# New order tables for the mixing work beside a gather-fed expert loop: tiles evicted one half later, taps by pairs of channel tiles, Silu, and sigmoids as tanh of half the argument

## The reference

```
xn = RMSNorm(x);  z = xn @ w_in -> u (512) | p, q (512 each) | gate logits (2048)
A  = GLU(gelu(S5 state-space layer(u)))            # GLU: pa * sigmoid(qa)
B  = silu(LayerNorm(causal depthwise conv of width 31 (p * sigmoid(q)))) @ w_conv_out
x  = x + (sigmoid(g_A) * A + sigmoid(g_B) * B) @ w_out
x  = x + PEER(RMSNorm(x))   # 8 heads; per token and head the 16 best of 128 x 128 experts:
                            # sum over the experts of softmax weight * gelu(u_e . x) * v_e
y  = RMSNorm(x)
```

## Time and profile before

| | |
|---|---|
| runs | 3581.5, 3581.9, 3587.0 us (median 3581.9) |
| the profiled execution | 3598.55 us, of which its span 3596.6 us |
| busy | PE 3197.2 us (89%), DVE 2433.1 (68%), ACT 1409.6 (39%), POOL 1401.1 (39%) |
| TensorE clock granted | 0.962 of full on the mean |
| moved by DMA | 1336.42 MB, 1140.92 MB of it gathers |
| ACT table loads | 1283 ns each; 94 in the group at L905 alone |

### The profile page before, as it was taken

How to read it: one execution, slowest core, us unless ns; L and a number is a source line. 1 busy time by engine, 2 the same in 40 slices (tenths; PEclk the granted TensorE clock), 3 DMA queues, 4 the chain that set the end, 5 groups by cost and what they waited for, 6 DMA issues and landing times.

```text
span 3596.6 us, 33769 instructions
## 1 busy us (share of the span) xinstructions
PE 3197.2 (89%) x10016; PEld 1828.4 (51%) x10016; DVE 2433.1 (68%) x5507; ACT 1409.6 (39%) x4197; POOL 1401.1 (39%) x1240
## 2 busy tenths in 40 slices
PE   7888999999999998999999998999999877777776
PEld 6676555555555555555655555555655322322232
DVE  6633579777656689777656588777666666666674
ACT  4312444554333344554333444554333333333332
POOL 1101445333343444333333344434333444454443
PEclk9899998999999998999999998999999999999999
DMA  4257998999999998999999997999999999999998
GB/s 135 72 169 239 380 418 334 367 419 379 419 405 417 410 405 321 376 410 389 419 405 404 404 407 291 389 409 400 419 409 405 409 420 420 394 420 414 414 403 348
DMA packets 232071, 1336.42 MB, mean 372 GB/s; under 512 B 27664, under 2 KB 49296, under 8 KB 92624
## 3 DMA queue, kind: packets, MB, share of 16 engines
q0 software_dynamic: 156672, 1140.92, 78.0%
q1 hardware_dynamic: 62992, 179.96, 13.7%
q10 hardware_dynamic: 12224, 13.38, 1.0%
HBM read 1310.93 MB, written 23.23 MB: 371 GB/s over the span
## 4 chain that ended last, share of the span: by engine, by line
PE 61%; DMA 20%; ACT 8%; DVE 5%; issue 5%; POOL 1%; POOLq 0%; SPq 0%; DVEq 0%; ACTq 0%
PE ps_acc L757 33%; DMA rows<-in_experts,idx 19%; PE ps_a L593 15%; PE ps_v L593 5%; PE ps_a L668 3%; DVE rows L1363 2%; ACT uy L814 2%; POOL rows L1509 1%; PE ps_y L635 1%; ACT coef L908 1%; ACT diag L912 1%; PE ps_a L695 1%; DVE va L1208 1%; ACT L905 1%; PE ps_a L672 1%
## 5 line engine op out<-in xcount | busy, mean ns | idle before, releaser
L757 PE MATMUL ps_acc<-rows,diag 128*128 128x512 f32 x4352 | 2052.8, 620 | 319.8 <-ACT diag L912 316.6
L1509 POOL DMA_INDIRECT rows<-in_experts,idx x1088 | 1272.5, 1170 | 1878.4 <-PE ps_acc L757 1516.9
L1363 DVE CUSTOM_DVE_ANT_0 rows<-rows,xn 128x1024 f32<-128x1024 f32 x1088 | 1331.1, 1233 | 845.8 <-DMA rows<-in_experts,idx 832.4
L757 PEld LDWEIGHTS ps_acc<-rows,diag 128*128 128x128 f32 x4352 | 839.9, 198 | 1370.3 <-issue 862.7
L905 ACT ACTIVATE act_v<-dots 128x2 f32<-128x2 f32 x544 | 109.8, 202 | 1170.0 <-DVE dots L1363 1158.2
L912 ACT ACTIVATE diag<-pk,coef 128x128 f32<-128x128 f32 x1088 | 377.2, 394 | 17.7
L593 PE MATMUL ps_a<-xnT,ring 128*128 128x272 f32 x1536 | 375.1, 400 | 0.9 <-ACT xnT L802 0.7
L593 PEld LDWEIGHTS ps_a<-xnT,ring 128*128 128x128 f32 x1536 | 297.5, 194 | 93.1 <-issue 35.0
L908 ACT ACTIVATE coef<-act_v,soft 128x1 f32<-128x1 f32 x1088 | 261.4, 287 | 17.8
L593 PE MATMUL ps_a<-gates,ring 128*128 128x272 f32 x1024 | 247.7, 395 | 4.2 <-issue 3.4
L1208 DVE SCALAR_TENSOR_TENSOR va<-va,pk 128x302 f32<-128x302 f32 x480 | 247.1, 579 | 1.9
(11 more groups left out here) (224 smaller groups left out, 2240.6 us busy)
## 6 DMA issues: line engine op xcount, KB each, us to landing
ring<-in_slabs SPq DMA_DIRECT2D x256, 512.0 KB
rows<-in_experts,idx POOLq DMA_INDIRECT x1088
ring<-made_slabs SPq DMA_DIRECT2D x24, 512.0 KB
sc<-score_rows SPq DMA_DIRECT2D x68, 128.0 KB
score_rows<-gp ACTq DMA_DIRECT2D x32, 256.0 KB
xt<-in_x_prompt SPq DMA_DIRECT2D x4, 1024.0 KB
x_rows<-xt ACTq DMA_DIRECT2D x4, 1024.0 KB, 11.6
x2t<-x_rows SPq DMA_DIRECT2D x8, 512.0 KB
```

The lines of the kernel that those rows point to most:

```text
L757: ins = pe.matmul(ps_acc[:, h, :], diag[:, slot, :], rows[:, slot, D + h * 512:D + (h + 1) * 512], start=first, stop=False, skip_group_che ...
L1363: ins = dve.tensor_tensor_reduce(rows[:, slot, 0:D], rows[:, slot, 0:D], xn[:, :], 1.0, 0.0, ALU.mult, ALU.add, dots[:, s:s + 1])
L1509: pool.indirect_dma_start(out=rows[:, slot, :], out_offset=None, in_=experts, in_offset=bass.IndirectOffsetOnAxis(ap=idx[:, a, k:k + 1], a ...
```

## The change

The two tables are rewritten and get a field `lag`, 0 for the opening, 1 for steady groups: ACT evicts `u`, `cq`, `gate`, `glu`, `out`, `q` and `score` tiles `lag` halves after PE made them. The taps are issued in 32 units of two taps on two of the four channel tiles, so that tiles 0 and 1 can start before `cp` 2 and 3 are there; no tap unit stands in a half that has a turn and scan. The S5 outputs are spread: three halves apart in the opening (before two), and at 20, 24, 32, 36 in a steady group (before 26, 28, 30, 32). `OPEN` is 59 instead of 60. Scores 0 are loaded one query slab earlier, scores 1 and the rows of the first tile one slab later.

Every sigmoid of the gates and of both GLUs becomes tanh(x/2): sigmoid(x) = (1 + tanh(x/2))/2. DVE forms (1 + tanh) times the other factor in one `scalar_tensor_tensor` in place of a `tensor_tensor`; the halves are taken up in conv_w, b_gate, norm_ffn, the `out` eviction, a factor 0.5 in the merge, and an identity times two (`eye2`) for the residual. The swish is one Silu on ACT, straight into `cs`, eight instructions a group, in place of four sigmoids on ACT and twelve instructions on DVE.

```diff
-    def __init__(self, pe, other, streamed):
-        self.pe, self.other = pe, other
+    def __init__(self, pe, other, streamed, lag):
+        self.pe, self.other, self.lag = pe, other, lag
...
@@ -108,36 +108,39 @@
 
 OPENING = Plan(
     {"xn": [0], "u": [1, 2, 3, 4], "cq": [5, 7, 9, 11], "cp": [6, 8, 10, 12],
-     "s": [10, 12, 14, 16], "y": [14, 16, 18, 20],
-     "gate": [13 + m for m in range(10)] + [31 + m for m in range(6)], "glu": [23 + j for j in range(DT)],
-     "mean": [32], "var": [34], "cout": [38, 39, 40, 41], "out": [43 + j for j in range(DT)],
-     "rows": [52, 53, 54], "q": [51 + m for m in range(2 * HEADS)],
-     "score": [52 + m for m in range(2 * HEADS)]},
+     "s": [10, 12, 14, 16], "y": [15, 18, 21, 24],
+     "gate": [13 + m for m in range(13)] + [34 + m for m in range(3)], "glu": [26 + j for j in range(DT)],
+     "mean": [29], "var": [32], "cout": [37, 38, 39, 40], "out": [42 + j for j in range(DT)],
+     "rows": [51, 52, 53], "q": [50 + m for m in range(2 * HEADS)],
+     "score": [51 + m for m in range(2 * HEADS)]},
     {"cp": [7, 9, 11, 13], "turn_in": [11, 13, 15, 17], "scan": [11, 13, 15, 17], "turn_back": [11, 13, 15, 17],
-     "gelu": [15, 17, 19, 21], "tap": [15 + k // 2 for k in range(TAPS)], "glu": [24 + j for j in range(DT)],
-     "centre": [33], "square": [33], "eps": [35], "root": [35], "scale": [36], "swish_in": [36], "swish": [37],
-     "cout": [39, 40, 41, 42], "rows": [53, 54, 55], "sq": [55], "ms2": [56], "rs": [57],
-     "load_x": [60], "sq_next": [64], "ms_next": [65], "norm_next": [66]}, False)
+     "gelu": [16, 19, 22, 25], "tap": [10, 10, 12, 12, 14, 14, 16, 16] + [18 + u // 2 for u in range(24)],
+     "glu": [27 + j for j in range(DT)],
+     "centre": [30], "square": [30], "eps": [33], "root": [33], "scale": [34], "swish": [35],
+     "cout": [38, 39, 40, 41], "rows": [52, 53, 54], "sq": [54], "ms2": [55], "rs": [56],
+     "load_x": [59], "sq_next": [63], "ms_next": [64], "norm_next": [65]}, False, 0)
 STEADY = Plan(
-    {"xn": [0], "u": [17, 19, 21, 23], "cq": [1, 5, 9, 13], "cp": [3, 7, 11, 15],
-     "s": [20, 22, 24, 26], "y": [26, 28, 30, 32],
-     "gate": [25 + 2 * m for m in range(10)] + [44] + [61 + 2 * m for m in range(5)],
+    {"xn": [0], "u": [9, 11, 21, 23], "cq": [1, 5, 13, 17], "cp": [3, 7, 15, 19],
+     "s": [12, 16, 24, 28], "y": [20, 24, 32, 36],
+     "gate": [25 + 2 * m for m in range(10)] + [44, 54] + [61 + 2 * m for m in range(4)],
      "glu": [45 + 2 * j for j in range(DT)],
-     "mean": [52], "var": [58], "cout": [71, 73, 75, 77], "out": [80 + 2 * j for j in range(DT)],
-     "rows": [95, 97, 99], "q": [96 + 2 * m for m in range(2 * HEADS)],
-     "score": [97 + 2 * m for m in range(2 * HEADS)]},
-    {"cp": [5, 9, 13, 17], "turn_in": [22, 24, 26, 28], "scan": [22, 24, 26, 28], "turn_back": [22, 24, 26, 28],
-     "gelu": [27, 29, 31, 33], "tap": [18 + k for k in range(TAPS)], "glu": [47 + 2 * j for j in range(DT)],
-     "centre": [54], "square": [55], "eps": [60], "root": [61], "scale": [62], "swish_in": [63], "swish": [65],
-     "cout": [73, 75, 77, 79], "rows": [97, 99, 101], "sq": [101], "ms2": [102], "rs": [104],
-     "load_x": [106], "sq_next": [117], "ms_next": [119], "norm_next": [121]}, True)
+     "mean": [48], "var": [54], "cout": [68, 70, 72, 74], "out": [77 + 2 * j for j in range(DT)],
+     "rows": [94, 96, 98], "q": [93 + 2 * m for m in range(2 * HEADS)],
+     "score": [95 + 2 * m for m in range(2 * HEADS)]},
+    {"cp": [6, 10, 18, 22], "turn_in": [14, 18, 26, 30], "scan": [14, 18, 26, 30], "turn_back": [14, 18, 26, 30],
+     "gelu": [21, 25, 33, 37],
+     "tap": [11, 12, 13, 15, 16, 17, 19, 20, 21, 22, 23, 24, 25, 27, 28, 29] + [31 + u for u in range(16)],
+     "glu": [48 + 2 * j for j in range(DT)],
+     "centre": [51], "square": [52], "eps": [57], "root": [58], "scale": [60], "swish": [62],
+     "cout": [70, 72, 74, 76], "rows": [96, 98, 100], "sq": [101], "ms2": [102], "rs": [104],
+     "load_x": [106], "sq_next": [117], "ms_next": [119], "norm_next": [121]}, True, 1)
...
 SKEW = 4
-OPEN = 60
+OPEN = 59
...
+        eye2 = sb("eye2", [P, P])
...
@@ -492,11 +495,11 @@
                     sp.wait_ge(made_stored, 96)
                 mix(h, 0)
 
-                if h == OPENING.pe["q"][5]:
-                    for b in range(2):
+                for b in range(2):
+                    if h == OPENING.pe["score"][2 * b + 1] + 2:
                         sp.wait_ge(score_out[b], 32)
                         load_scores(0, b)
-                if h == OPENING.pe["q"][7]:
+                if h == OPENING.pe["q"][8]:
                     sp.wait_ge(rows_out, 32)
                     sp.wait_ge(rs_out, 48)
                     load_rows(0)
...
 
             def mix(h, g):
-                at, due = plan(g).at, plan(g).due
-                for _ in at("xn", h):
+                due = plan(g).due
+
+                def at(piece, h):
+                    return plan(g).at(piece, h - plan(g).lag)
+
+                for _ in plan(g).at("xn", h):
                     to_channels(a_at(g, "xn"), "norm_mix", g)
                 for m in at("u", h):
                     cross(uS[:, m, :], ready(a_at(g, "u", m)), ACT.Copy, False).then_inc(a_done, 1)
                 for j in at("cq", h):
                     if j >= 2:
                         v_emptied(v_at(g, "cp", j - 2))
-                    act.activation(sig[:, j % 2, :], ready(a_at(g, "cq", j))[:, 0:N], ACT.Sigmoid).then_inc(a_done, 1)
+                    act.activation(sig[:, j % 2, :], ready(a_at(g, "cq", j))[:, 0:N], ACT.Tanh, scale=0.5).then_inc(a_done, 1)
                 for m in at("gate", h):
-                    act.activation(gates[:, m, :], ready(a_at(g, "gate", m))[:, 0:N], ACT.Sigmoid,
-                                   bias=par("b_gate")[:, m:m + 1]).then_inc(a_done, 1)
+                    act.activation(gates[:, m, :], ready(a_at(g, "gate", m))[:, 0:N], ACT.Tanh,
+                                   bias=par("b_gate")[:, m:m + 1], scale=0.5).then_inc(a_done, 1)
...
-                for _ in due("swish_in", h):
+                for _ in due("swish", h):
+                    act.wait_ge(y_done, CT * (g + 1) + 2)
                     act.wait_ge(ln_ready, g + 1)
                     for c in range(CT):
-                        act.activation(sq[:, c, :], acc[:, c, :], ACT.Sigmoid, bias=par("ln_b")[:, c:c + 1],
-                                       scale=par("ln_g")[:, c:c + 1]).then_inc(ln_sig, 1)
+                        out, shape = by_step(cs[:, c, :]), (par("ln_b")[:, c:c + 1], par("ln_g")[:, c:c + 1])
+                        act.activation(out[:, :, 0:KP], in_time(acc[:, c, 0:NP]), ACT.Silu, bias=shape[0], scale=shape[1])
+                        act.activation(out[:, :, KP:NK], in_time(acc[:, c, SOFF:NC]), ACT.Silu, bias=shape[0],
+                                       scale=shape[1]).then_inc(cs_ready, 1)
...
             def setup_angle():
 
                 dve.wait_ge(kept_in, 16)
-                dve.tensor_copy(tails[:, :, HALO:2 * HALO], par("cache").rearrange("p (c k) -> p c k", c=CT))
+                dve.tensor_scalar(tails[:, :, HALO:2 * HALO], par("cache").rearrange("p (c k) -> p c k", c=CT), 2.0, None, ALU.mult)
+                dve.tensor_scalar(par("conv_w"), par("conv_w"), 0.5, None, ALU.mult)
+                dve.tensor_scalar(par("b_gate"), par("b_gate"), 0.5, None, ALU.mult)
+                dve.tensor_scalar(par("norm_ffn"), par("norm_ffn"), 0.5, None, ALU.mult)
+                dve.tensor_scalar(eye2[:, :], par("eye"), 2.0, None, ALU.mult)
...
-            def tap(k):
-
-                taps = par("conv_w")
-                for c in range(CT):
-                    src, wk = vbuf[:, c, k:k + NC], taps[:, c * TAPS + k:c * TAPS + k + 1]
-                    if k == 0:
-                        before[c] = mark(dve.tensor_scalar(acc[:, c, :], src, wk, par("conv_b")[:, c:c + 1],
-                                                           ALU.mult, ALU.add))
-                    else:
-                        after(before[c])
-                        last = dve.scalar_tensor_tensor(acc[:, c, :], src, wk, acc[:, c, :], ALU.mult, ALU.add)
-                        if k < TAPS - 1:
-                            before[c] = mark(last)
-                if k == TAPS - 1:
+            def tap(unit, g):
+
+                taps, (two, first) = par("conv_w"), divmod(unit, 16)
+                if first == 0:
+                    emptied(v_at(g, "cp", 2 * two + 1))
+                for k in range(2 * first, min(2 * first + 2, TAPS)):
+                    for c in (2 * two, 2 * two + 1):
+                        src, wk = vbuf[:, c, k:k + NC], taps[:, c * TAPS + k:c * TAPS + k + 1]
+                        if k == 0:
+                            before[c] = mark(dve.tensor_scalar(acc[:, c, :], src, wk, par("conv_b")[:, c:c + 1],
+                                                               ALU.mult, ALU.add))
+                        else:
```

(30 more changed lines are left out.)

23 lines of the change are left out of this document (12 added, 11 removed).

## The result

The changed kernel takes 3492.5 us (median of 4 runs, 3491.4 to 3493.2) against 3581.7 us (median of 4 runs, 3570.3 to 3587.0): a ratio of 0.9755, 95% interval 0.9731 to 0.9778. Forecast were 3505 us and a range of 3474 to 3546. The profiled execution took 3491.98 us, of which its span is 3489.9 us. Lines of the changed file are higher by 3 to 17: L593 is L596, L757 is L760, L814 is L817, L845 is L852, L905 is L915, L1363 is L1375, L1509 is L1521.

The account below looks back on a forecast made before the run. A PE chain bounds the opening to the first gather, then transfers, with three dents where the DMA engines idle. Opening 34 us plus dents 43 us make 77 off 3581.9: 3505 us, range 3474 to 3546.

Parts of the forecast that it names:

- the likeliest case: The forecast itself, with shorter opening and shallower dents in the steady groups: 3485 to 3520 us, chance 57%.
- (1): Opening, gates and outputs 1 to 3: outputs three halves apart cut PE's waits; 22 us won, bounds 13 and 30.
- (2): Opening, LayerNorm: four slabs between `var` and `cout` leave 1.0 us of wait; 9 us won, bounds 5 and 10.
- (3): Opening: scores 0 loaded one slab earlier, 3.7 us won; first tile's rows a slab later cost 0, at worst 2.
- (4): Opening: four more small DVE instructions before the first normalisation, minus 0.9 us.
- (5): Steady groups: lag 1 and spread outputs end the gelu wait; y turn 14.0 us on PE, no PSUM bank missing.
- (6): Steady groups: DVE's taps overrun in turns with a scan; 6 us a group remain, at worst 12, at best none.
- the DVE rival: DVE stays the limit in the dents, 16 us of each remain: 3535 us, chance 15%.
- the slower one: Taps alternating between two channel tiles wait on each other, decisive from 0.78 us a tap: 3650 us, chance 8%.
- (7): DVE's `scalar_tensor_tensor` for `tensor_tensor`: 0 to 0.1 us on 48 instructions, offset by 12 swish instructions that go.
- (8): Silu holds ACT for about 2.9 us and two loads, hidden by the transfers.
- the loads stay: Tanh shares no table set with gelu, so each gelu keeps its 1.28 us load: 3521 us, chance 18%.

Follow-up runs that it names:

- the run with all three: Changed kernel with three opening edits: gate 12 in half 26, inverse roots and first rows earlier, silu at half 34 instead of 35; 3469.2 us, ratio 0.9681.

## Why the prediction was right, and where its sizes were off

**The sum.** 3505 us forecast, 3492.5 measured: sign, size and the likeliest case hold, but by two errors of opposite sign, 10 us too much for the opening and 22 too little for what comes behind it. That they came to 12 together was luck. The lower end of the range, 3474, lies 4 us below what its own terms give (43 and 61 off 3581.9 are 3478).

**(1) Gates and outputs, 22 forecast, 18 measured.** `glu` 0 starts at 156.02 behind thirteen gate slabs, before at 163.27 behind ten: 7.3 + 3 x 3.68 = 18.3 us. The waits came as worked out. The clock was mis-sized: 2 us were set aside, and behind output 1 alone it cost 3.3 (17.7 us to output 2, where output 2 to 3 takes 14.4); another 2.7 came behind this step's end, in `glu` 0. One load stayed, 1.4 us, since the tanh before the first gelu ran from a set without gelu.

**(2) LayerNorm, 9 forecast, 3 measured.** The wait before `cout` fell from 7.6 us to 2.5, not to 1.0: the wrong term is the silu's price, 0.72 us for a pair, from rows of other shapes, where a pair takes some 1.05. `cout` fell from 16.99 to 16.55 us and not to 14.7, since the clock fell again. The wait alone does not explain that: behind the same 2.47 us `cout` took 14.93 us with the gate moved and with Sigmoid. And 2.7 us of the 5.1 won in the wait were lost ahead of it, in the slow matmuls of `glu` 0 (4.00 + 2.70 us for what takes 2.00 + 2.00).

**(3) Scores 3.7, (4) setup minus 0.9: 2.8 forecast, 3.0 measured** (`out` starts 21.3 us earlier, the first gather 24.3), within what its place varies. But the rows of the first tile, which the same step put at 0, at worst 2, cost some 8 (8.5 us behind the first gather in the run that moves them alone, 8.3 in the run with all three). The step said that the next user waits for a gather too. The rows show that it did not: the first dot, at 325.25, waits for no gather, only for the normalisation, and this for the small load, which took 14.75 us beside the gathers. It is the step that failed outright.

**(5) Lag and outputs.** The y turn was right: 13.2 us from 579.67 to 592.89, against 14.0 forecast and 19.0 before; a turn that has an `s` piece beside the y piece takes 15.0 (524.05 to 539.05). No steady output waits for its gelu any more. The clock did not stay everywhere: the turn before the one shown has a wait of 4.09 us for diagonals and takes 16.3 us, and the share of the stretch is 1.01 all the same. A bank was missing for long only once: of the 15.2 us that PE's slabs from `gates` ever wait, 14.4 are the one wait at 325.25, for an eviction of ACT, which stood before the load of the inverse roots for 15.6 us. These rows are from PE's timeline:

```profile
524.05 3.83 PE L596 MATMUL ps_a<-xnT,ring 128*128 128x272 f32 x16
...
539.05 3.83 PE L596 MATMUL ps_a<-xnT,ring 128*128 128x272 f32 x16
...
579.67 3.83 PE L596 MATMUL ps_a<-xnT,ring 128*128 128x272 f32 x16
...
592.89 3.83 PE L596 MATMUL ps_a<-xnT,ring 128*128 128x272 f32 x16
```

What was wrong is the frame: "what happens elsewhere to ACT, DVE or PE is hidden under transfers, whose bytes don't change". The lag is worth 67 us, and a third of it lies in halves with a share of 1.01. That ACT's place costs time there is measured (23 us); by what path is argued only: a later diagonal means a later free slot and so a later transfer. Nor is all of it hidden from the share. The packets of all queues took 94.9% of the span in the repetition of the changed kernel and 94.5% in the run without the lag of `out`, `q` and `score`, 3312 and 3318 us: of the 21 us between the two profiles some 6 are longer packets and 15 idle engines, each good to some 7 us. Spread over three groups, idle time of that size hardly stands out in any one window.

**(6) Taps and scans.** The residue of 6 us a group is not to be seen: the shares of the dents are 0.99 to 1.01. The row of the taps says 584 ns, before 579; so the DVE rival (15%) is out, and so is the slower one (8%), whose chain over two tiles would have shown as 0.78 us and more. The old halves with the lag cost 19 us: spreading was worth less than the lag. The prediction had put a price on neither alone.

**(7), (8)** were not taken out one by one, so that they cost nothing is not shown.

**The rival "the loads stay" (18%)** fell with its premise. ACT's table loads, from the groups of instructions:

```profile
L915 ACT ACT_TABLE_LOAD x40 | 51.3, 1283 | 2.8 <-DVE dots L1375 2.1
L907 ACT ACT_TABLE_LOAD x34 | 43.6, 1283 | 0.6
...
L817 ACT ACT_TABLE_LOAD x1 | 1.3, 1283 | 0.0
```

87 in all, before 240. Once gelu's set is loaded (104.47), gelu follows tanh without a load, and tanh follows Silu without one (205.58), so in this build tanh is in the sets of both. The Trainium skill ("ScalarE: Activation LUTs", section on table sets) lists tanh with exp and with sigmoid, and gelu as a set of its own. For the step from tanh to gelu that is not the whole list, and the trace decides. What loads at every gelu would have meant for the time was measured with Sigmoid: 4 to 9 us, and not the 16 of that rival, as loads under transfers cost nothing that can be measured (3189.5 us from the first gather, against 3186.8).

**Open.** The packets of all queues took 92.9% of 3596.6 us before, 3341 us, and 94.9% of 3489.9 after, 3312 us, for the same bytes. So of the 107 us between the two profiles some 77 are less idle time and 29 are shorter packets. (The shares are rounded to 0.1% for each queue, so such a figure is good to some 7 us.) The two runs with lag 0 have 3334 and 3344 us, the lag on the kernel before 3325, and all the others between 3308 and 3322: the shorter packets go largely with the lag. By what means was not tested. Open are also what besides a wait decides whether PE's clock falls, and 8 to 13 us that the rest of the edit costs.

## What to carry to other kernels

In a stream in order, evict a product one step after the step that makes it: an engine that waits for its own step's product holds up everything queued behind it. Here this was worth 67 us with the rest of the change in place, and some 40, for four of the pieces, without it. Don't take a DMA share near 1 as proof that waits are free; compare the GB/s of two traces over the same work and the share of the whole run, and take the wait away as a trial. And small loads belong ahead of the first burst of gathers, even if their user seems to wait for the gathers too.

## What the runs showed of the hardware

- Tanh needs no table load behind gelu or Silu, nor gelu behind such a tanh (the first gelu behind tanh, at 104.47 us, did need one); 87 loads in place of 240, 1283 ns each.
- A load issued 4.5 us behind the first of eight gathers of 1 MB landed after 14.75 us; issued 1.4 us ahead of them it was there before DVE was ready for it, 10 us later.
- The same 1336 MB took between 3308 and 3344 us of packet time in 14 profiles with the same transfers (each figure good to some 7 us).
- After a PE wait of 4.1 us eight matmuls of 272 columns took 4.00 us, after one of 0.46 us 2.10 us. But the length of the wait alone does not settle it: behind 4.13 us they took 2.8 us in two other runs, and behind a wait of 2.47 us the 64 matmuls of `cout` took 16.5 to 16.6 us in eight runs with this opening and 14.93 in two.
